# Hybrid block with PEER experts: GpSimd makes the low part of every other weight unit in the choice stage

## The reference, cut

```
h = x + W_out( concat[ sigmoid(g) * FoX(qn,kn,v,f), StickBreak(q,k,v) ] )     from RMSNorm(x)
xn = RMSNorm(h)
q  = xn @ w_pq                                      8 heads, 2 halves of 128
s  = q . sub_keys                                   128 keys for each half
top 16 of each half -> 256 sums -> top 16 -> idx, g = softmax
act = gelu( xn . u[idx] )                           16384 experts, rows of 2048
y  = h + sum over the 128 chosen of  g * act * v[idx]
```

## Time and profile before

| | |
|---|---|
| three runs | 3232.72, 3235.67, 3231.48 us |
| span of the profiled execution | 3235.6 us; the profile states no other time for it; the nearest of the runs is 3235.67 |
| PE busy | 3205.5 us, 99% |
| DVE busy | 2229.6 us, 69% |
| ACT busy | 1115.4 us, 34% |
| POOL busy | 944.2 us, 29% |
| granted clock of TensorE | 1.00 in every stretch |
| moved by DMA | 778 MB, 240 GB/s over the span, 302 to 332 GB/s in the middle of the choice stage |

### The profile page before, as it was taken

The page is one execution under the profiler, slowest core; times in us unless marked ns, Lnnn a source line. Parts: engine busy times, 40 slices in busy tenths (PEclk is TensorE's granted clock), DMA queues, the critical chain, the costliest instruction groups (busy, mean ns, idle before and its releaser), DMA issues. The chain is left out here.

```text
span 3235.6 us, 40909 instructions
## 1 busy us (share of the span) xinstructions
PE 3205.5 (99%) x16666; PEld 2808.9 (87%) x16666; DVE 2229.6 (69%) x2637; ACT 1115.4 (34%) x1156; POOL 944.2 (29%) x425
## 2 busy tenths in 40 slices
PE   8999999999999999999999999999999999999999
PEld 6887777888878899999999899889889988888887
DVE  3016665112037898888875898888888888888887
ACT  4123333444242134655643232232223233222221
POOL 4433333233333321111101233233323321223222
PEclk9999999999999999999999999999999999999999
DMA  3222222122333246899867999889989998898988
GB/s 144 94 102 78 78 75 80 67 74 109 126 124 117 91 171 248 302 324 332 321 225 294 343 346 349 331 330 357 350 321 343 356 340 305 317 338 340 344 321 312
DMA packets 171380, 778.11 MB, mean 240 GB/s; under 512 B 14064, under 2 KB 80752, under 8 KB 86384
## 3 DMA queue, kind: packets, MB, share of 16 engines
q1 hardware_dynamic: 127488, 457.77, 38.7%
q0 software_dynamic: 43776, 318.79, 26.2%
HBM read 731.10 MB, written 44.34 MB: 240 GB/s over the span
## 5 line engine op out<-in xcount | busy, mean ns | idle before, releaser
L405 ACT ACTIVATE wh<-raw 128x2048 fp32r<-128x2048 f32 x343 | 656.3, 1913 | 1057.3 <-PE bank L452 867.7
L425 PE MATMUL bank<-xh,wh 128*128 128x336 f32 (+1 forms) x2928 | 1004.4, 343 | 0.0
L427 PE MATMUL bank<-xh,wl 128*128 128x336 f32 (+1 forms) x2928 | 990.4, 338 | 0.0
L426 PE MATMUL bank<-xl,wh 128*128 128x336 f32 (+1 forms) x2928 | 988.5, 338 | 0.0
L1142 DVE TENSOR_TENSOR wl<-raw,wh 128x2048 fp32r<-128x2048 f32 x252 | 576.6, 2288 | 205.9 <-ACT wh L405 205.4
L411 POOL TENSOR_TENSOR wl<-raw,wh 128x2048 fp32r<-128x2048 f32 x92 | 424.5, 4614 | 722.7 <-ACT wh L405 722.5
L426 PEld LDWEIGHTS bank<-xl,wh 128*128 128x128 f32 x2928 | 550.8, 188 | 35.3 <-issue 1.9
L425 PEld LDWEIGHTS bank<-xh,wh 128*128 128x128 f32 x2928 | 550.4, 188 | 35.1 <-issue 1.9
L427 PEld LDWEIGHTS bank<-xh,wl 128*128 128x128 f32 x2928 | 549.7, 188 | 35.0
L450 PE MATMUL bank<-wh,xh 128*128 128x512 f32 x1328 | 517.4, 390 | 0.3 <-DVE wl L1142 0.3
L452 PE MATMUL bank<-wh,xl 128*128 128x512 f32 x1328 | 517.0, 389 | 0.0
(11 more groups left out here) (209 smaller groups left out, 2740.6 us busy)
## 6 DMA issues: line engine op xcount, KB each, us to landing
raw<-in_u SPq DMA_DIRECT2D x128, 1024.0 KB
raw<-in_v SPq DMA_DIRECT2D x128, 1024.0 KB
raw<-in_w_in SPq DMA_DIRECT2D x56, 1024.0 KB
gate_scratch<-arena SPq DMA_DIRECT2D x12, 2048.0 KB
arena<-gate_scratch SPq DMA_DIRECT2D x32, 768.0 KB, 9.2
raw<-in_w_out SPq DMA_DIRECT2D x16, 1024.0 KB
raw<-in_w_pq SPq DMA_DIRECT2D x16, 1024.0 KB
act_scratch<-arena SPq DMA_DIRECT2D x68, 168.0 KB
```

Source lines behind the costliest of these rows:

```text
L405: nc.scalar.activation(wh[s][:], raw[s][:], ACT.Copy).then_inc(hi_done, 1)
L425: nc.tensor.matmul(dst, w_h[:, c], xh[:, c, 0:width], start=(c == 0), stop=False)
L426: nc.tensor.matmul(dst, w_h[:, c], xl[:, c, 0:width], start=False, stop=False)
L427: last = nc.tensor.matmul(dst, w_l[:, c], xh[:, c, 0:width], start=False, stop=(c == KC - 1))
```

## The change

`LO_POOL = range(11, 64, 2)`: the low parts of the units 11, 13, ..., 63 of the choice stage (27 units) are made by POOL with `split_lo`, and DVE's `lo` is left out for them. In POOL's program they are put between the gathers: at step k first `split_lo` of unit k+1 if k+1 is in the list, then the gathers that wait for the dots of step k. Since two engines now make low parts in turn, `lo_done` becomes two semaphores, one for each buffer, and all who wait for it (SP, PE, ACT, POOL, DVE) wait for the one of their unit with half the count.

```diff
+LO_POOL = range(11, 64, 2)
...
-        lo_done = sem("lo_done")
+        lo_done = [sem(f"lo_done{s}") for s in range(2)]
...
+        def low_part(eng, k, i=0, stride=0):
+
+            eng.wait_ge(lo_done[k % 2], k // 2 + 1 + (stride // 2) * i)
+
...
-                sp.wait_ge(lo_done, k - 1 + stride * i)
+                low_part(sp, k - 2, i, stride)
...
-                                    ALU.subtract).then_inc(lo_done, 1)
+                                    ALU.subtract).then_inc(lo_done[s], 1)
...
-            pe.wait_ge(lo_done, k + 1 + stride * i)
+            low_part(pe, k, i, stride)
...
-            for j in range(PN + NB):
+            def pair_gather(j):
+
                 if j >= 2:
                     pool.wait_ge(pair_used, j - 1)
...
+            for j in range(2):
+                pair_gather(j)
+            for k in range(DOT_UNITS[0], N_PROUNITS):
+                if k + 1 in LO_POOL:
+                    split_lo(pool, N_PRO + k + 1)
+                for j in range(2, PN + NB):
+                    if DOT_UNITS[j - 2] == k:
+                        pair_gather(j)
...
             for k in range(8, GATE_FROM):
-                lo(N_PRO + k + 1)
+                if k + 1 not in LO_POOL:
+                    lo(N_PRO + k + 1)
...
             for k in range(GATE_FROM, N_PROUNITS):
                 ahead = GATE_STEP * (k - GATE_FROM) + 2
-                lo(N_PRO + k + 1)
+                if k + 1 not in LO_POOL:
+                    lo(N_PRO + k + 1)
```

More of the change, by code:

```diff
@@ L520, in norm_gemm @@
                 turn_chunk(pe, z, c, range(DB, TB))
-            pe.wait_ge(lo_done, k + 1)
+            low_part(pe, k)
             if m >= 2:
@@ L794, in _ @@
             nc.gpsimd.tensor_copy(wh[1][:], raw[1][:]).then_inc(hi_done, 1)
-            pool.wait_ge(lo_done, 1)
+            low_part(pool, 0)
             split_lo(pool, 1)
@@ L869, in _ @@
                 hi_chunk(act, 0, c)
-            act.wait_ge(lo_done, 2)
+            low_part(act, 0)
+            low_part(act, 1)
             def forget_act():
@@ L1142, in lo @@
                 nc.vector.tensor_tensor(wl[k % 2][:], raw[k % 2][:], wh[k % 2][:].bitcast(F32),
-                                        ALU.subtract).then_inc(lo_done, 1)
+                                        ALU.subtract).then_inc(lo_done[k % 2], 1)
             nc.vector.tensor_copy(wh[0][:, 0:512], zeros).then_inc(forget_step, 1)
@@ L1158, in _ @@
                                     raw[0][:, 0:KC * PH].rearrange("p (c e) -> p c e", e=PH),
-                                    forget_w[:, :, 0:PH].bitcast(F32), ALU.subtract).then_inc(lo_done, 1)
+                                    forget_w[:, :, 0:PH].bitcast(F32), ALU.subtract).then_inc(lo_done[0], 1)
             dve.wait_ge(const_loaded, 16 * 5)
@@ L1490, in hot @@
                 last.then_inc(hot_done, 1)
-            dve.wait_ge(lo_done, LO_DVE)
+            low_part(dve, LO_DVE - 2)
+            low_part(dve, LO_DVE - 1)
             def pair_index():
```

## The result

| | before | after |
|---|---|---|
| median (range), four runs each | 3232.1 us (3230.62 to 3235.67) | 3275.24 us (3275.01 to 3279.06) |
| ratio, 95% interval | | 1.0136 [1.0122, 1.015] |
| span of the profiled execution | 3235.6 us | 3273.7 us |

The change costs 43 us. The forecast was +15, and its range ended at 3266. All the loss lies in the choice stage. From the first matmul of unit 0 to that of unit 67, matmul starts in the trace give 585.7 us before and 628.1 after: +42.4. (The two profiled spans differ by 38.1 alone: the traced execution of the kernel before is the slowest of its four, and 4.3 us longer outside this stage.)

A forecast was written before the change was run, and what follows sets the result against it. PE was taken as the bound, busy 3205.5 of 3235.6 us. Terms 5 + 1 + 8 + 2.5 + 2 = 18.5, less 3.6 of today's waits, gave +15 on 3232.7: 3248 us, range 3236 to 3266.

The forecast's parts named there:

- POOL's queue: Units 11 and 13: low parts stand behind gathers that wait for dots; 4 us plus about 1, together 5.
- lookups: Units 16 to 19 and 54 to 57: lookups in place of a dot put DVE over its time; 1 us for both.
- 20 to 39 (net of today's 3.6): Doubled steps: DVE 188 us against PE's 174, taken as 8 us; 3.6 us of today's waits at units 30 to 34 subtracted.
- 40 to 51: Choice stage: DVE's work with holds 114 us against 110; between 0 and 4 us, taken as 2.5.
- ACT's late high parts: Odd units 19 + 4m, now POOL's: late high parts have 2.1 us of room, before 4.4; taken as 2 us.
- Semaphores: Same number of waits, one more on ACT and DVE each, once; no cost.
- length of the chain: From end of unit k-2 to start of unit k: POOL's low part of 4.6 us fits and alone costs nothing.
- The hold: Each POOL low part shuts out DVE's `hot`, dots, lookups and low parts for 4.6 us.
- DVE's budget: DVE's work per two units, 12.2 us or 16.8 with the hold, of PE's 18.36; about 3 us ahead of need.
- the rival in which DVE is the bound: Rival 2: no slack helps, waits of gathers add fully, late dots delay PE again; +28 us, 3261; chance 0.15.
- PE waits for DVE's tables and not for POOL's low parts: Sign that the forecast is wrong and DVE is the bound; the forecast expected PE waits for POOL's low parts.
- Late loads: Rival 3: SP issues loads 2.3 us later for 27 units; 9 us above the forecast, 3257; chance 0.08.

The follow-up runs named there:

- Taking it away: The change with the low parts of units 11, 13 and 15 back on DVE, POOL's from unit 17 on; 3269.4 us, 6 below the change.
- every run of the table: Twelve follow-up kernels listed beside the change, each with ratio to the kernel before, PE's gap growth and stage growth; ratios 1.0002 to 1.0161.
- the moved hold: The change, but POOL begins each odd unit's low part only when DVE has made the second table of the unit before; 3261.37 us.
- the three subsets: The change with only 15, 2 (units 19 and 57) or 11 of the 27 low parts on POOL; 3245.8, 3237.34 and 3243.72 us.
- the run with the first three alone: The change with only the low parts of units 11, 13 and 15 on POOL; 3240.11 us, ratio 1.0025.

## Why the prediction was wrong in size

The direction and the mechanism (POOL's low part shuts DVE out) were right, the sum was a third of the loss. The growth of the stage, by the prediction's own pieces:

| units | forecast, us | measured, us |
|---|---|---|
| 10 to 15, POOL's queue | 5 | 5.2 |
| 16 to 19, lookups | 1 | 4.1 |
| 20 to 39 (net of today's 3.6) | 4.4 | 14.0 |
| 40 to 51 | 2.5 | 14.9 |
| 54 to 57, lookups | (in the 1 above) | 3.9 |
| ACT's late high parts | 2 | in the rows above, 2.97 at unit 31; 0.4 behind unit 58 |

- **Queue: right.** The gather took 1.68 us, POOL's low part 4.82, and the wait was 3.62, between the 2.7 and 4.8 named. Taking it away gave 6 us.
- **Semaphores, length of the chain: right.** The low part of 4.60 us starts 2.36 us after the unit before last wherever nothing is late, and PE waits at 5 of 27 units.
- **The hold: right,** and now shown for the table instructions: L1501 1.10 to 6.05 us. The Trainium skill (GPSIMD Engine Reference, Key points) names the contention; that here it lasts as long as POOL works is what the rows show. The run with four pieces shows that cutting the work into shorter instructions, back to back, doesn't soften it.
- **DVE's budget: the step that failed.** "DVE runs about 3 us ahead of its need" let a surplus of one pair pay for the next, and the averages (16.8 of 18.36 us, "if the waits for gathers fall into the holds, none") gave 8 and 2.5. As an average the 3 us were fair: in the kernel before, PE wants the second table 6.43 us into a unit, and it was finished 3.9 us ahead of that in the mean of the even units, but between 6.4 ahead and 0.9 late. But tables have two buffers: DVE can't be further ahead than PE's last batch, and what it gains in odd units it waits out (14.4 us at L1488). What counts is where DVE stands at one moment, when POOL's low part begins, 2.4 to 5.8 us into each even unit. In the late ones it had just waited for a gather, made a second dot or looked up numbers. If the second table is finished, the hold costs PE no wait for it, and if it isn't, 2 to 4 us. The prediction also left out that POOL's queue ties the two: the gather in front of the low part waits for the dot in front of the table. Units 40 to 51, where I had counted 114 us of work against 110, lost 14.9.
- **TensorE's clock: a term that was missing.** I priced a wait at its own length. The gaps grew by 27.6 us, the stage by 42.4. Of the 14.8 between, about 12 to 13 are matmuls at a lower granted clock, 0.72 in six microseconds around and behind the end of each of the waits of the units 18, 26, 31, 38, 46 and 56, 0.53 behind 50; the rest are delays under 0.25 us beside the waits. In every run of the table whose gaps grew by more than 2 us the stage grew by 1.3 to 1.6 times the gaps, and each has at least one such slow stretch. In some it is the smaller part: with the gathers left out, the clock is low behind unit 18 alone and takes under 2 of the 4.4 us between. Without this, the change would have given 3232.1 + 28 = 3260, near the rival in which DVE is the bound (3261) and inside the range; that would have been luck in part, since the waits for tables were not those that I had summed.
- **Rivals.** "PE waits for DVE's tables and not for POOL's low parts" was named as what would make DVE the bound: it came, with 23.4 against 7.6 us. I gave it 15% and priced it by its work, not by its moment. And what the sign was to show is not so: DVE isn't the bound, since it still waits for PE and ACT (14.4 and 1.4 us in 1300 to 1480) and is busy for 88% there. Late loads didn't come: PE waits for none. ACT's waits even fell, from 17.3 and 4.9 to 10.0 and 2.9:

```profile
ACT arena L1095 <- DMA gate_scratch<-arena: 10.0, 3, 5.2
ACT wh L410 <- DMA raw<-in_u: 2.9, 2, 1.9
```

**What stays open.** No run here is faster than the kernel before, and none was tried with a third table buffer, which the argument above names as what would let DVE be ahead; so that step is argued from the wait at L1488 and from the moved hold, not shown by its removal. Nor was one tried in which the low part stands in front of the gather in POOL's queue, which would tell that order from DVE's waits for gathers. Nor is the selection of units settled: the three subsets show that a choice made from one trace is no choice for the next.

## What to carry to other kernels

Work given to an engine that looks free can cost its neighbour the whole duration, if the two shut each other out: look at what the neighbour is doing at the moment when the new work starts, in each unit, and not at its busy share. Look also at whether one event releases both. An engine whose outputs are double-buffered can't save time up, so a sum over many units tells little about one late table in one of them. Where PE is the bound at a granted clock of 1.00, a new wait of 2 us and more can cost more than its length: here the stage grew by about one and a half times the waits.

## What the runs showed of the hardware

- In these traces DVE and POOL shut each other out for whole instructions. POOL's low part of 4.60 us becomes 6.59 behind a dot of 2.28; DVE's four TENSOR_SCALAR of 1.10 us become 6.05 beside it, and stay at 6.46 when POOL's work is cut in four.
- The granted clock falls behind some waits and not behind others of the same length. In the changed kernel (length, busy PE, clock, DMA share, GB/s), around or behind the end of the waits of unit 11 (3.62 us), 31 (2.97), 34 (2.52) and 50 (3.95):

```profile
1229.00:1235.00 6.00, 4.92 (x32) 1.00 0.64 203
...
1419.00:1425.00 6.00, 5.28 (x27) 0.72 0.73 240
1457.00:1463.00 6.00, 5.15 (x36) 1.00 0.58 203
...
1622.00:1628.00 6.00, 5.74 (x23) 0.53 0.53 175
```

A clock of 0.50 is the lower of TensorE's two levels (1.2 of 2.4 GHz), and the stretches of 0.72 are part at one and part at the other. In the run with the first three alone the same wait of 3.62 us at unit 11 was followed by 1.5 us of slow matmuls, in the changed kernel by none to speak of. What decides it, these runs don't tell.
